# RMS norms in a two-layer diffusion backbone: the last square summed by TensorE, and the roots spread with the identity as moving operand

## The chip, the cores and the metric

The kernel runs on one core of one Trainium2 chip. The metric is the device time of one execution in microseconds (us), lower is better.

## The reference, cut to what matters

The reference is a two-layer backbone over 512 latent tokens and 256 context tokens of 1024 features. Layer 0 mixes tokens with multi-scale retention (4 heads), layer 1 with neighbourhood attention (latent tokens only at its end), and each layer ends in a gated convolutional feed-forward network. What this change touches are the norms:

```
def _rmsnorm(x, w):
    y = x * rsqrt(mean(x * x, axis=-1, keepdims=True) + NORM_EPS)
    return y * w

h  = _rmsnorm(x, norm1_w[i]) * (1 + sc1) + sh1        # before the mixer, each layer
h2 = _rmsnorm(x, norm2_w[i]) * (1 + sc2) + sh2        # before the feed-forward, each layer
o  = o * rsqrt(mean(o * o, axis=-1) + NORM_EPS)       # in retention, once per head
return _rmsnorm(x, final_norm_w)                      # the output
```

That is nine norms: one at the start, four in the retention heads, and four of the residual stream further on.

## The kernel before, in words

Features lie on the partitions and tokens along the free axis, so `x` is 8 tiles of 128 features by 768 tokens (512 latent, then 256 context), and only the 512 latent columns are worked on from the attention's output projection on. A norm has to add squares over all 1024 features of a token, which is a sum over tiles and then over partitions.

All five queues are written out by hand, with semaphores between them. TensorE multiplies weights that arrive as 512 KB chunks. Each chunk is split by ScalarE (`w_hi`, line 804) and VectorE (`w_lo`, line 1169) into a high and a low part, and every product is three matmuls (high by high, high by low, low by high), in the format fp32r. The norm's own matmuls are plain fp32, and one such matmul shows as two weight loads and two matmuls in the trace.

A norm of the residual stream runs so:

1. When TensorE has finished output tile m (0 to 7), VectorE adds it to `x` (`add_gated`, line 1336, or line 1722 in the attention), ScalarE squares it (`final_square`, line 842, into `S[m % 2]`), and VectorE adds the square to `ss` (`add_square`, line 1195). Between these, both engines split a weight chunk for the next products.
2. After the eighth square is added, TensorE multiplies each 128-token block of `ss` with two columns of ones (`token_sums`, line 427), so that a token's sum stands on the token's own partition: `sums`, 2 columns per block, in the fourth bank of `o_ps`.
3. ScalarE takes the square root (`root`, line 830). Ahead of it a dummy activation (line 827) loads the table, so that the load doesn't wait for the sums.
4. VectorE takes the reciprocal (`one_over`, line 1201) and multiplies it into copies of the identity (line 1202), which makes `ss` a row of 128x128 diagonal matrices, 6 or 4 of them.
5. TensorE multiplies ones (128x128, stationary) by these diagonals (`spread_roots`, line 434): a matmul of 512 columns and, where context is included, one of 256. Every partition then holds the root of every token (`spread`).
6. VectorE multiplies `x` by it (line 1313, or 1734 in the final norm), ScalarE adds the shift and rounds (line 873), VectorE makes the low part (line 1322), and the first tile of the next products can start (line 448).

The four norms of this kind are called A (after retention's output projection), B (after the first feed-forward), C (after the attention's output projection, 512 tokens) and D (the output's, 512 tokens). The start norm and the four head norms use `add_squares` for all squares and the same steps 2 to 5. In a head, step 5 stands inside a running product: TensorE does it ahead of the fourth of eight blocks of `project_at(0, ...)`. At the start, ScalarE copies `spread` back to `ss` (line 848), and VectorE alternates between dot products for the modulation (lines 1216, 1218) and the norm's work.

In the first feed-forward VectorE also makes the second layer's modulation vectors (`ada_step`, line 1285, one or two after each output tile; `take_ada`, line 1292).

Of the kernel before, what the change touches and what calls it, by code (L numbers as in the profile page):

```python
# [37 lines left out]
P = 128  # L38
# [98 lines left out]
def backbone(nc, x_in, weights, ada_first, ada, cond_rows, small_in, bias_in, masks_in, park, out):  # L137
    ctx = ExitStack()
    with ctx:
# [99 lines left out]
        sq_done, sq_added = sem("sq_done"), sem("sq_added")  # L239
        sums_done, root_done, diag_done, spread_done = sem("sums_done"), sem("root_done"), sem("diag_done"), sem("spread_done")  # L240
        norm_t, h_hi_done, h_lo_done = sem("norm_t"), sem("h_hi_done"), sem("h_lo_done")
# [117 lines left out]
        def _(pe):  # L359
# [70 lines left out]
            def spread_roots(parts):  # L430

                pe.wait_ge(diag_done, diags.up())
                for c0, cn, _ in parts:
                    mm = nc.tensor.matmul(spread[:, c0:c0 + cn], ones[:, :], ss[:, c0:c0 + cn], start=True, stop=True)  # L434
                mm.then_inc(spread_done, 1)

            def project_two(parts, ready, tiles=None):
# [327 lines left out]
            out_projection(True)  # L765
            token_sums(KC, TOK)
            spread_roots(PARTS)
            ffn(PARTS)
            token_sums(KC, TOK)
            spread_roots(PARTS)  # L770
# [10 lines left out]
            h_split.up(KC)  # L781
            token_sums(KC, LAT)
            spread_roots(LATENT)
            ffn(LATENT)
            token_sums(KC, LAT)
            spread_roots(LATENT)
# [3 lines left out]
        def _(act):  # L790
# [187 lines left out]
            def ffn(layer, parts, ends):  # L978
                width = parts[-1][0] + parts[-1][1]
                for n, size in enumerate(GROUPS):  # L980
# [19 lines left out]
                    for m in range(2):  # L1000
                        t, after = wait_after()
                        split()
                        if last:
                            final_square(t, after, 0, m, width)
                    pairs = 2 if ends and last else 3
                    with turns(act, pairs, A.steps(2) + [(raws[0], 16), (raws[1], 16), (squares_added, 2 * last)]) as i:
                        for m in range(2):
                            t, after = wait_after()
                            split()
                            if last:  # L1010
                                final_square(t, after, 2 * i + 2, m, width)
                    if pairs == 2:
                        for m in range(2):
                            t, after = wait_after()
                            final_square(t, after, 6, m, width)

# [134 lines left out]
        def _(dve):  # L1151
# [45 lines left out]
            def one_over(width):  # L1197

                t = width // P
                dve.wait_ge(root_done, roots.up())  # L1200
                step(nc.vector.reciprocal(rms[:, 0:t], rms[:, 0:t]))
                nc.vector.tensor_tensor(ss[:, 0:width].rearrange("p (t q) -> p t q", q=P),
                                        ident.rearrange("p (t q) -> p t q", t=1).to_broadcast([P, t, P]),
                                        rms[:, 0:t].rearrange("p (t q) -> p t q", q=1).to_broadcast([P, t, P]),
                                        ALU.mult).then_inc(diag_done, 1)

# [134 lines left out]
            def out_projection(with_ada, first_ada=0, final=False):  # L1341
                if final:
                    step(nc.vector.memset(ss[:, :], 0.0))
                own_done()
                for m in range(KC):
                    add_gated(m, 0, 16, PARTS)
                    if m % 2:
                        split()
                    if final:
                        add_square(m % 2, TOK)  # L1350
                    if m % 2:
                        if m < 2 * with_ada:
                            ada_step(first_ada + m // 2, S[3])

            def rotated(j):
# [145 lines left out]
            def ffn(layer, parts, with_ada, ends):  # L1501
# [4 lines left out]
                for n, size in enumerate(GROUPS):  # L1506
# [33 lines left out]
                    own_done()  # L1540
                    pairs = 2 if ends and n == 2 else 3
                    last = n == len(GROUPS) - 1
                    if last:
                        step(nc.vector.memset(ss[:, :], 0.0))
# [16 lines left out]
                    with turns(dve, pairs, A.steps(2) + steps) as i:  # L1561
# [7 lines left out]
                        if loads:  # L1569
                            take_ada(1, i * loads + nj, loads, conds)  # L1570
                    nj += 3 * loads
                    if pairs == 2:
                        for m in range(2):
                            add_gated(6 + m, layer, 40, parts)
                            add_square(m, w_all)

# [10 lines left out]
            head_attention(0, True)  # L1587
            steps = [(ada_loads, 128), (hi_splits, 16), (own_steps, 19), (squares_made, VC), (ada_made, 8), (decays, 4)]
            steps += [(v_hi_made, TT), (qk_hi_made, 8), (p_hi_made, 7), (gate_hi_made, 4)]
# [126 lines left out]
            for m in range(KC):  # L1716
                if m in (0, 4):
                    dve.wait_ge(x_back[m // 4], 16)
                t, tile = out_tile(m)
                wait_at(t)  # L1720
                xv = x[:, m, 0:LAT].rearrange("p (r c) -> p c r", c=COLS)
                nc.vector.scalar_tensor_tensor(xv, tile.rearrange("p (c r) -> p c r", r=ROWS), mod[:, 1, 16 + m, 0:1], xv,
                                               ALU.mult, ALU.add).then_inc(acc_taken[t], 1)
                if m >= 3:
                    split()
                add_square(m % 2, LAT)
            pads()
# [155 lines left out]
```

## Time and profile before

| | |
|---|---|
| median of 3 runs | 2078.77 us (2076.61 to 2079.49) |
| the profiled execution | 2078.47 us |
| its span, first to last instruction | 2076.4 us |
| mean granted TensorE clock | 0.979 of full |
| TensorE busy | 1982.3 us, 95% of the span |
| VectorE busy | 1342.3 us, 65% |
| ScalarE busy | 755.6 us, 36% |
| GpSimd busy | 97.1 us, 5% |

The 2.07 us between the span and the execution's time lie ahead of and behind the instructions. The granted clock is 1.00 at 2.4 GHz and 0.50 at 1.2 GHz. Times in the rows count from the start of the span.

### The profile page before, as it was taken

The page shows a single profiled execution, that of the slowest core. Times are in us where ns is not written, and L with a number is a line of the kernel's source. Part 1 is how long each engine was busy: PE and PEld are TensorE (multiplying, and loading weights), DVE is VectorE, ACT ScalarE, POOL GpSimd, SP SyncE. Part 2 cuts the span into 40 slices and gives each one's busy share as a digit, 9 for nine tenths or more (in the row PEclk, how much of TensorE's full clock was granted, in tenths as well). Part 3 has the DMA queues.
Part 4 walks back from the last instruction along what each step waited for, and adds up shares of the span by engine and source line. Part 5 has one row for each costly group of instructions (what it writes and reads, how often), then busy time and mean ns, then how long its engine had stood idle before and what let it go on. Part 6 is the DMA issues. An engine that isn't in the chain of part 4 may idle for free.

```text
span 2076.4 us, 29858 instructions
## 1 busy us (share of the span) xinstructions
PE 1982.3 (95%) x10452; PEld 1687.3 (81%) x10452; DVE 1342.3 (65%) x2251; ACT 755.6 (36%) x1281; POOL 97.1 (5%) x162
## 2 busy tenths in 40 slices
PE   5999999999999889999999999899999889999997
PEld 4878888888888778888888887688888768788785
DVE  7866635735745677766664667777877667557375
ACT  4423223223313344312321233456556444333232
POOL 0000000000000000000000000311111000000000
PEclk8999999999999989999999999899999989999999
DMA  7221311321221112233224334211111222223222
GB/s 291 90 83 62 112 61 52 106 68 62 92 81 61 61 59 93 91 132 105 97 101 132 101 101 152 89 46 42 56 45 35 92 71 94 98 91 101 91 91 101
DMA packets 51256, 186.39 MB, mean 90 GB/s; under 512 B 5680, under 2 KB 5680, under 8 KB 51184
## 3 DMA queue, kind: packets, MB, share of 16 engines
q1 hardware_dynamic: 37744, 136.73, 19.4%
q0 software_dynamic: 13440, 48.63, 7.0%
q8 instruction: 53, 0.87, 0.2%
q14 instruction: 19, 0.16, 0.0%
HBM read 181.15 MB, written 4.19 MB: 89 GB/s over the span
## 4 chain that ended last, share of the span: by engine, by line
PE 83%; DVE 9%; issue 4%; ACT 3%; DMA 1%; DVEq 0%; SPq 0%; ACTq 0%
PE acc L393 58%; PE o_ps L483 3%; PE o_ps L518 3%; PE acc L606 3%; PE acc L483 2%; PE o_ps L649 2%; PE acc L664 2%; PE acc L505 2%; PE acc L448 2%; PE o_ps L664 2%; DVE pt_lo L1625 1%; PE acc L639 1%; PE o_ps L434 1%; PE acc L699 1%; DVE w_lo L1169 1%
## 5 line engine op out<-in xcount | busy, mean ns | idle before, releaser
L804 ACT ACTIVATE w_hi<-raw 128x1024 fp32r<-128x1024 f32 x232 | 245.2, 1057 | 597.5 <-PE acc L393 477.6
L1169 DVE TENSOR_TENSOR w_lo<-raw,w_hi 128x1024 fp32r<-128x1024 f32 x232 | 284.2, 1225 | 275.4 <-ACT w_hi L804 273.9
L393 PE MATMUL acc<-h_hi,w_hi 128*128 128x512 f32 x1520 | 437.5, 351 | 4.9 <-DVE w_lo L1169 3.4
L393 PE MATMUL acc<-h_hi,w_lo 128*128 128x512 f32 x1520 | 434.5, 349 | 0.0
L393 PE MATMUL acc<-h_lo,w_hi 128*128 128x512 f32 x1520 | 434.1, 349 | 0.0
L393 PEld LDWEIGHTS acc<-h_hi,w_hi 128*128 128x128 f32 x1520 | 245.2, 188 | 44.4 <-ACT u L990 4.2
L393 PEld LDWEIGHTS acc<-h_lo,w_hi 128*128 128x128 f32 x1520 | 245.0, 188 | 39.6
L393 PEld LDWEIGHTS acc<-h_hi,w_lo 128*128 128x128 f32 x1520 | 243.9, 188 | 38.7
L1336 DVE SCALAR_TENSOR_TENSOR x<-acc,mod,x 128x512 f32<-128x512 f32 (+3 forms) x136 | 81.9, 637 | 145.1 <-PE acc L393 135.7
L393 PE MATMUL acc<-act_hi,w_lo 128*128 128x512 f32 (+1 forms) x396 | 119.8, 356 | 0.0
L393 PE MATMUL acc<-act_hi,w_hi 128*128 128x512 f32 (+1 forms) x396 | 119.5, 356 | 0.0
L393 PE MATMUL acc<-act_lo,w_hi 128*128 128x512 f32 (+1 forms) x396 | 119.3, 355 | 0.0
L1285 DVE CUSTOM_DVE_ANT_0 ada_raw<-ada_raw,silu_rows 128x1024 f32<-128x1024 f32 x80 | 97.9, 1223 | 4.9 <-DMA ada_raw<-in_ada_dram 2.8
L312 POOL DMA_DIRECT2D ada_raw<-in_ada_dram x79 | 41.8, 529 | 1180.0 <-DVE mod_new L1285 1180.0
L997 ACT ACTIVATE act_hi<-scratch 128x768 f32 (+1 forms) x44 | 32.5, 740 | 154.2 <-DVE scratch L1529 154.2
L1520 DVE SCALAR_TENSOR_TENSOR scratch<-u,taps,scratch 128x769 f32<-128x769 f32 (+1 forms) x88 | 78.0, 887 | 3.1
L1522 DVE SCALAR_TENSOR_TENSOR scratch<-u,taps,scratch 128x769 f32<-128x769 f32 (+1 forms) x88 | 78.0, 887 | 3.1
L1625 DVE TENSOR_TENSOR pt_lo<-acc,pt_hi 128x256 fp32r<-128x256 f32 (+1 forms) x128 | 52.3, 450 | 35.3 <-ACT pt_hi L1065 35.2
L393 PEld LDWEIGHTS acc<-act_lo,w_hi 128*128 128x128 f32 x396 | 65.0, 187 | 12.1
L393 PEld LDWEIGHTS acc<-act_hi,w_lo 128*128 128x128 f32 x396 | 65.0, 187 | 12.0
L393 PEld LDWEIGHTS acc<-act_hi,w_hi 128*128 128x128 f32 x396 | 65.0, 187 | 11.9
L1535 DVE TENSOR_TENSOR act_lo<-scratch,act_hi 128x768 f32 (+1 forms) x44 | 36.3, 825 | 45.4 <-ACT act_hi L997 45.4
(231 smaller groups left out, 3520.5 us busy)
## 6 DMA issues: line engine op xcount, KB each, us to landing
raw<-in_weights_dram SPq DMA_DIRECT2D x232, 512.0 KB, 3.3
ada_raw<-in_ada_dram POOLq DMA_DIRECT2D x80, 512.0 KB, 3.6
ada_start<-in_ada_first_dram SPq DMA_DIRECT2D x8, 1024.0 KB, 18.3
x<-in_x_in_dram SPq DMA_DIRECT2D x4, 768.0 KB, 7.0
park_dram<-x POOLq DMA_DIRECT2D x1, 2048.0 KB, 8.1
rel<-in_bias_dram POOLq DMA_DIRECT2D x16, 128.0 KB, 2.4
x<-park_dram POOLq DMA_DIRECT2D x2, 1024.0 KB, 6.6
out_dram<-x SPq DMA_DIRECT2D x8, 256.0 KB, 2.1
```

Of the source, the lines that this page charges most:

```text
L393: mm = nc.tensor.matmul(tile[:, c0:c0 + cn], wt[:, b * P:(b + 1) * P], mv[:, n, c0:c0 + cn], start=(n == 0 and m == 0), stop=(n == last an ...
L483: mm = nc.tensor.matmul(tile, hs[:, k, t * P:(t + 1) * P], ws[:, d * RV:(d + 1) * RV], start=(k == 0 and m == 0), stop=(last and m == 2))
L518: mm = nc.tensor.matmul(tile, vt[:, c0:c0 + P], pt[i % 2][:, p0:p0 + qn], start=((context or i == 0) and n == 0 and m == 0), stop=(i >= 5 ...
L606: mm = nc.tensor.matmul(tile[:, c0:c0 + cn], wt[:, n * P:(n + 1) * P], mv[:, n, c0:c0 + cn], start=(n == 0 and m == 0), stop=(n == size - ...
L664: mm = nc.tensor.matmul(tile[:, c0:c0 + cn], wt[:, n * P:(n + 1) * P], mv[:, n, c0:c0 + cn], start=(n == 0 and m == 0), stop=(n == KC - 1 ...
L804: nc.scalar.activation(w_hi[i][:, :], raw[i][:, :], ACT.Copy).then_inc(hi_split, 1)
L1169: nc.vector.tensor_tensor(w_lo[i][:, :], raw[i][:, :], w_hi[i][:, :].bitcast(F32), ALU.subtract)\
L1285: nc.vector.tensor_tensor_reduce(ada_raw[:, :], ada_raw[:, :], silu_rows[:, 0, :], 1.0, 0.0, ALU.mult, ALU.add, mod_new[:, j, 0:1]).then_i ...
L1336: ins = nc.vector.scalar_tensor_tensor(xv, tile[:, c0:c0 + cn], mod[:, layer, bass.ds(gate + m, 1), c:c + 1].rearrange("p a c -> p (a c)") ...
L1520: step(nc.vector.scalar_tensor_tensor(S[j][:, 0:width], u[j][:, 1:1 + width], tap(1), S[j][:, 0:width], ALU.mult, ALU.add))
L1522: nc.vector.scalar_tensor_tensor(S[j][:, 0:width], u[j][:, 2:2 + width], tap(2), S[j][:, 0:width], ALU.mult, ALU.add).then_inc(conv_done, 1)
L1625: ins = nc.vector.tensor_tensor(lo, tile[:, c0:c0 + zn * P].rearrange("p (t q) -> p t q", q=P), hi.bitcast(F32), ALU.subtract)
```

## The change: what it does

In norms A to D the eighth square is no longer added to `ss`. The new `final_sums` takes the place of `token_sums`: TensorE waits for seven additions and multiplies `ss` with ones (first batch, 6 or 4 matmuls), and then waits for ScalarE's eighth square and multiplies `S[1]` with ones on top, into the same PSUM columns (second batch, as many again). TensorE itself raises `sq_added` in place of the addition that went.

In all nine norms the diagonals are gone. `spread_roots` waits for the reciprocal alone, and does one matmul for each 128-token block: stationary is the block's column of reciprocals, repeated 128 times by a stride of zero, moving is the 128x128 identity. The columns multiplied are as many as before (768 or 512), in 6 or 4 matmuls in place of 2 or 1.

In the last group of both feed-forwards, output tiles 6 and 7 are written out behind the loop, in VectorE's and ScalarE's queues alike, with the same steps in the same order but for the addition that went.

```diff
             def spread_roots(parts):
-                pe.wait_ge(diag_done, diags.up())
-                for c0, cn, _ in parts:
-                    mm = nc.tensor.matmul(spread[:, c0:c0 + cn], ones[:, :], ss[:, c0:c0 + cn], start=True, stop=True)
+                pe.wait_ge(roots_ready, diags.up())
+                for t in range((parts[-1][0] + parts[-1][1]) // P):
+                    mm = nc.tensor.matmul(spread[:, t * P:(t + 1) * P], rms[:, t:t + 1].to_broadcast([P, P]), ident,
+                                          start=True, stop=True)
                 mm.then_inc(spread_done, 1)
+
+            def final_sums(width):
+                pe.wait_ge(sq_added, squares_added.up(KC) - 1)
+                for t in range(width // P):
+                    mm = nc.tensor.matmul(sums[:, 2 * t:2 * t + 2], ss[:, t * P:(t + 1) * P], ones[:, 0:2],
+                                          start=(t == 0), stop=False)
+                mm.then_inc(sq_added, 1)
+                pe.wait_ge(sq_done, squares_added.now())
+                for t in range(width // P):
+                    mm = nc.tensor.matmul(sums[:, 2 * t:2 * t + 2], S[1][:, t * P:(t + 1) * P], ones[:, 0:2],
+                                          start=False, stop=(t == width // P - 1))
+                mm.then_inc(sums_done, 1)
...
-            token_sums(KC, TOK)
+            final_sums(TOK)
             spread_roots(PARTS)
...
                 dve.wait_ge(root_done, roots.up())
-                step(nc.vector.reciprocal(rms[:, 0:t], rms[:, 0:t]))
-                nc.vector.tensor_tensor(ss[:, 0:width].rearrange("p (t q) -> p t q", q=P),
-                                        ident.rearrange("p (t q) -> p t q", t=1).to_broadcast([P, t, P]),
-                                        rms[:, 0:t].rearrange("p (t q) -> p t q", q=1).to_broadcast([P, t, P]),
-                                        ALU.mult).then_inc(diag_done, 1)
+                nc.vector.reciprocal(rms[:, 0:t], rms[:, 0:t]).then_inc(roots_ready, 1)
...
-                    if final:
+                    if final and m < KC - 1:
                         add_square(m % 2, TOK)
...
-                    pairs = 2 if ends and n == 2 else 3
+                    pairs = 2 if last else 3
...
-                    if pairs == 2:
+                    if last:
                         for m in range(2):
                             add_gated(6 + m, layer, 40, parts)
-                            add_square(m, w_all)
+                            if not ends:
+                                split()
+                            if m == 0:
+                                add_square(m, w_all)
+                            if loads:
+                                ada_step(m, waste, conds)
```

## Rows read from the trace of the kernel before

**Rows 1.** Page, part 4: the chain that ended last, share of the span by engine.

```profile
PE 83%; DVE 9%; issue 4%; ACT 3%; DMA 1%; DVEq 0%; SPq 0%; ACTq 0%
```

**Rows 2.** Instructions on `ss`: engine, count, duration in ns (min/median/max), span, forms.

```profile
L1195 DVE TENSOR_TENSOR ss<-ss,scratch x32: 681/822/959, 693.9 to 2063.2; 128x768 f32<-128x768 f32 x16, 128x512 f32<-128x512 f32 x16
```

**Rows 3.** Chain in order of time, norm A: start us, us, what.

```profile
718.60 1.12 DVE x L1336 x2
...
720.83 0.96 DVE ss L1195
...
721.84 2.73 PE o_ps L427 x12
...
724.59 0.19 ACT rms L830
...
725.10 0.97 DVE ss L1202
...
726.11 2.94 PE o_ps L434 x4
...
732.77 7.31 PE acc L448 x25
```

**Rows 4.** Timeline, norm A: start us, us, engine, what [idle before <-releaser].

```profile
716.50 0.96 DVE L1195 TENSOR_TENSOR ss<-ss,scratch 128x768 f32<-128x768 f32 x1 [0.96 <-ACT scratch L842]
...
720.64 1.28 ACT L827 ACT_TABLE_LOAD   x1
```

**Rows 5.** Timeline, norm B.

```profile
1293.69 0.84 ACT L842 ACTIVATE scratch<-x 128x768 f32 x1 [0.52 <-DVE x L1336]
...
1297.30 0.17 DVE L1300 SCALAR_TENSOR_TENSOR norm_a<-mod,small 128x16 f32<-128x16 f32 x1 [0.28 <-DVE mod L1292]
...
1300.03 2.93 PE L434 MATMUL o_ps<-ss,ones 128*128 128x512 f32 x4 [1.73 <-DVE ss L1202]
```

**Rows 6.** Timeline, norm C, and then norm D.

```profile
1680.60 1.28 ACT L827 ACT_TABLE_LOAD   x1
...
1684.10 2.07 PE L434 MATMUL o_ps<-ss,ones 128*128 128x512 f32 x2 [1.27 <-DVE ss L1202]
...
2063.16 1.28 ACT L827 ACT_TABLE_LOAD   x1
...
2066.27 2.08 PE L434 MATMUL o_ps<-ss,ones 128*128 128x512 f32 x2 [1.30 <-DVE ss L1202]
```

**Rows 7.** Chain in order of time, start norm.

```profile
21.70 2.94 PE o_ps L434 x4
```

**Rows 8.** Timeline of the first head's norm, weight loads.

```profile
165.50 1.42 PEld L427 LDWEIGHTS o_ps<-ones,ss 128*128 128x128 f32 x12
...
169.27 0.30 PEld L393 LDWEIGHTS acc<-h_lo,w_hi 128*128 128x128 f32 x2
...
169.62 0.31 PEld L393 LDWEIGHTS acc<-h_hi,w_lo 128*128 128x128 f32 x2
...
170.96 0.19 PEld L434 LDWEIGHTS o_ps<-ss,ones 128*128 128x128 f32 x1 [0.24 <-issue]
171.39 0.19 PEld L434 LDWEIGHTS o_ps<-ss,ones 128*128 128x128 f32 x1 [0.24 <-issue]
171.60 0.41 PEld L393 LDWEIGHTS acc<-h_hi,w_hi 128*128 128x128 f32 x2
```

**Rows 9.** Timeline, a group of transposes in the attention.

```profile
1348.02 0.71 PE L639 MATMUL acc<-small,prob 128*128 128x128 f32 x5
```

**Rows 10.** Windows: stretch, us, busy us (x count) of PE, PEld, DVE, ACT, POOL, clock, DMA, GB/s.

```profile
28.00:29.00 1.00, 1.00 (x9) 1.00 (x9) 1.00 (x1) 0.00 (x0) 0.00 (x0) 0.77 1.03 410
...
721.00:722.00 1.00, 0.16 (x1) 0.16 (x1) 0.92 (x8) 0.99 (x2) 0.00 (x0) 0.72 0.00 0
...
738.00:739.00 1.00, 1.00 (x7) 0.85 (x6) 1.00 (x3) 0.70 (x2) 0.00 (x0) 0.74 0.00 0
...
1683.00:1684.00 1.00, 0.00 (x0) 0.00 (x0) 0.82 (x2) 0.04 (x1) 0.00 (x0) 1.00 0.92 365
```

More of the change, by code:

```diff
@@ L239, in backbone @@
         sq_done, sq_added = sem("sq_done"), sem("sq_added")
-        sums_done, root_done, diag_done, spread_done = sem("sums_done"), sem("root_done"), sem("diag_done"), sem("spread_done")
+        sums_done, root_done, roots_ready, spread_done = sem("sums_done"), sem("root_done"), sem("roots_ready"), sem("spread_done")
         norm_t, h_hi_done, h_lo_done = sem("norm_t"), sem("h_hi_done"), sem("h_lo_done")
@@ L765, in _ @@
             out_projection(True)
-            token_sums(KC, TOK)
+            final_sums(TOK)
             spread_roots(PARTS)
             ffn(PARTS)
-            token_sums(KC, TOK)
+            final_sums(TOK)
             spread_roots(PARTS)
@@ L781, in _ @@
             h_split.up(KC)
-            token_sums(KC, LAT)
+            final_sums(LAT)
             spread_roots(LATENT)
             ffn(LATENT)
-            token_sums(KC, LAT)
+            final_sums(LAT)
             spread_roots(LATENT)
@@ L1004, in ffn @@
                             final_square(t, after, 0, m, width)
-                    pairs = 2 if ends and last else 3
+                    pairs = 2 if last else 3
                     with turns(act, pairs, A.steps(2) + [(raws[0], 16), (raws[1], 16), (squares_added, 2 * last)]) as i:
@@ L1353, in out_projection @@
                             ada_step(first_ada + m // 2, S[3])
+                if final:
+                    squares_made.up()
             def rotated(j):
@@ L1540, in ffn @@
                     own_done()
-                    pairs = 2 if ends and n == 2 else 3
                     last = n == len(GROUPS) - 1
+                    pairs = 2 if last else 3
                     if last:
@@ L1570, in ffn @@
                             take_ada(1, i * loads + nj, loads, conds)
-                    nj += 3 * loads
-                    if pairs == 2:
+                    nj += pairs * loads
+                    if last:
                         for m in range(2):
                             add_gated(6 + m, layer, 40, parts)
-                            add_square(m, w_all)
+                            if not ends:
+                                split()
+                            if m == 0:
+                                add_square(m, w_all)
+                            if loads:
+                                ada_step(m, waste, conds)
+                        if loads:
+                            take_ada(1, nj, loads, conds)
+                        nj += loads
+                        squares_made.up()
             def pads():
@@ L1587, in _ @@
             head_attention(0, True)
-            steps = [(ada_loads, 128), (hi_splits, 16), (own_steps, 19), (squares_made, VC), (ada_made, 8), (decays, 4)]
+            steps = [(ada_loads, 128), (hi_splits, 16), (own_steps, 18), (squares_made, VC), (ada_made, 8), (decays, 4)]
             steps += [(v_hi_made, TT), (qk_hi_made, 8), (p_hi_made, 7), (gate_hi_made, 4)]
@@ L1725, in _ @@
                     split()
-                add_square(m % 2, LAT)
+                if m < KC - 1:
+                    add_square(m % 2, LAT)
+            squares_made.up()
             pads()
```

## The prediction

> **What bounds the kernel now.** I read the page first: TensorE, busy 95% of the span by the table above, holds 83% of the chain that ended last, VectorE 9% [rows 1]. So time is won only where TensorE stands still or does less, and VectorE's 9% are where it stands still. Next I listed the instructions on `ss`, the tile that the edit touches: four of 32 additions close a norm [rows 2], and all nine diagonals stand between a root and a spread. Then I read the chain at each norm. In norm A it is a relay with no slack: the eighth addition, 12 weight loads and matmuls for the sums, root, reciprocal, diagonals, spread [rows 3]. From the last product, which released VectorE at 718.60, to the end of the spread at 729.05 TensorE does nothing but these small matmuls, the later ones at half clock: the 12 of the sums take 2.73 us, where the same 12 in a head take 1.42 [rows 3, 8], and the granted clock fell in the window 721 to 722, at 721.44 by its mean of 0.72 [rows 10].
>
> **The prices.** A weight load with a matmul of two columns costs 1.42 / 12 = 0.118 us at full clock and 2.63 / 12 = 0.219 at half (the 2.73 less the last matmul's tail) [rows 3, 8]. The new spread does 12 loads, each with 128 moving columns, which the trace before doesn't show in plain fp32. Its matmul part follows from the old spread: loads 170.96 and 171.39 are one 512-column matmul apart, 0.43 us, so 128 columns are 0.107, or 0.213 at half clock [rows 8]. The load is the longer of the two. If it runs under the matmul ahead of it, 12 cost 12 x 0.118 = 1.42 us (0.219 each, 2.63, at half clock); if the two follow one another, 12 x 0.225 = 2.70 (5.18). I take the first. Transposes of the same shape, a load and 128 fp32 columns, stand (0.71 - 0.27) / 4 = 0.11 us apart, with 0.27 for the last one's own duration [rows 9]. And the old spread's third load went in at 170.96 just as the second matmul began.
>
> A rule speaks against this. The Trainium skill, "TensorE: Matmul & The Clock Gate", section "Measured speedup vs the span model", has weight loads overlapping with matmuls in flight "only when row_grp differs", and here all use the whole array. By that the second price would hold; this trace's rows for transposes speak for the first. I keep it as a rival below.
>
> **The change part by part.** Each term is a shift of the moment at which the spread is ready, against the profiled execution.
>
> *Start norm.* VectorE goes from the reciprocal to the diagonals (the size of A's, 0.97 us [rows 3]), TensorE's spread of 2.94 starts at 21.70 [rows 7], and ScalarE's copy and all that follows hang on it. The spread runs at the half-clock pace and stays at it: 12 x 0.219 + 0.3 for the tail = 2.93. The gain is the diagonal, 0.95. It is kept: the chain goes on from the spread through ScalarE's copy and then through VectorE, which has work without a gap for the rest of this norm. Between 0.9 and 1.0.
>
> *Heads, four times.* The product's weight loads come 0.35 us apart per pair (169.27, 169.62), so the next would be at 169.97. It came at 171.60: 1.63 us for the wait on the diagonals and the spread [rows 8]. The old wait ended by 170.5; without the diagonal it would end at about 169.5, before TensorE comes by. There is no wait left, and 1.42 for the loads: 0.21 saved, 0.85 over four heads. Ends 0.6 and 1.0, for loads 0.005 us further apart or closer.
>
> *First batch of the sums.* In A the seventh addition ended at 717.46, before the last product, which released VectorE at 718.60 [rows 3, 4]; the order in B, C and D is the same. The batch takes 1.42 (C and D 0.94) on an engine that waits for the eighth square anyway. In A that ends where the table load begins, 720.64 [rows 4]. Nothing is paid; without that cover it would be 1.42.
>
> *Norm A, addition and sums.* The second batch starts when the square ends, at some 720.7, not at 721.84. Its price depends on when the clock falls. At the old moment (721.44, from the 0.72) it does about six at 0.118 and six at 0.219, 2.0, and the root starts at 722.75 in place of 724.59. ScalarE allows 722.15: table load from 720.64 to 721.92, then the dummy's 0.2 [rows 4]. From root to spread there were 0.48 us for root and reciprocal, 0.97 for the diagonals and 0.04; now 0.53. Spread at 723.3 in place of 726.11 [rows 3]: 2.8 saved, and the spread itself is a draw at half clock. Ends: second batch wholly slow, 2.1; all at full clock, root 722.15, spread at 722.7 and 1.7 long in place of 2.94, 4.6.
>
> *Norm B.* The square ends at 1294.53. The batch needs about 2.3 with the clock falling soon after its start: root 1297.0, spread 1297.55 in place of 1300.03 [rows 5], 2.5 saved. A new limit lies close: VectorE still has its modulation step, now 0.96 earlier since the addition ahead of it is gone, and ends line 1300 at 1296.5 in place of 1297.47 [rows 5]. The reciprocal is queued behind it. This binds only if the sums run at full clock. Ends 2.2 and 4.4.
>
> *Norms C and D.* Here ScalarE binds: square, table load, dummy, root. The load ends at 1681.88 and 2064.44, the root can start 0.2 later, at 1682.1 and 2064.65, and the batch (8 x 0.118 = 0.94 behind a square that ends as the table load starts) is done by then. Spreads start at 1682.65 and 2065.2 in place of 1684.10 and 2066.27 [rows 6]: 1.45 and 1.05. Both old spreads ran at half clock (2.07, 2.08 us). The new ones are 8 x 0.118 + 0.3 = 1.24 if they come before the fall and 2.05 if after. At the old phase both would be fast: in C the granted clock was 1.00 through the window 1683 to 1684 [rows 10], in which the new one ends, and in D the old one starts 0.1 us after the new one ends. But A's fall at 721.4, 2.8 us after its product, shows that the phase differs. I take one of the two as fast: 1.45 + 1.05 + 0.83 = 3.3. Ends 2.5 and 4.15.
>
> The rest costs nothing: the written-out tiles 6 and 7 have the same steps, and ScalarE's and VectorE's splits for the next products lie where they did. Nothing waits anew on GpSimd or SyncE; their transfers are released by the same events, a few us earlier.
>
> **Sum.** 0.95 + 0.85 + 2.8 + 2.5 + 3.3 = 10.4 us. The profiled execution would go from 2078.47 to 2068.1; it stands 0.3 under the median, so the median would go from 2078.77 to 2068.4. The low ends add up to 0.9 + 0.6 + 2.1 + 2.2 + 2.5 = 8.3 (2070.5), the high ends to 1.0 + 1.0 + 4.6 + 4.4 + 4.15 = 15.2 (2063.6).
>
> **The rivals.**
>
> *Weight loads and matmuls in series.* In every spread each record costs 0.107 more at full clock and 0.213 at half: start, A and B 36 x 0.213 = 7.7, C and D 16 x 0.213 = 3.4, heads 48 x 0.107 = 5.1; 16.2 in all. 10.4 saved less 16.2 is 5.8 lost: 2084.6, slower. It eats the whole gain from 64% of that price on (10.4 of 16.2), and is slower by 0.2% from 90% on. For it speaks only that no plain fp32 load with 128 columns is in the trace, and that its operand is one column repeated; against it stand the transposes [rows 9]. That overlap which the skill's section denies is this rival.
>
> *The clock does not fall.* TensorE works wide again about 4.4 us after its last product, not 7.5 us. If that is enough in A, B, C and D, the terms reach their high ends, 2063.6. The products after the norm would also start at full clock. In A they began at 732.77 and the clock rose only in the window 738 to 739, at 738.5 by its mean of 0.74 [rows 3, 10]: of 5.7 us half is lost, 2.9. VectorE, which makes the tiles in step with them, would keep about half of that back; 1.5 remain in A and as much in C: down to 2060.6. Against it: two-column matmuls did not hold the clock at the start, where it fell in the window 28 to 29 with TensorE busy throughout [rows 10], and from the spread's end to the products another 3.7 us went by (729.05 to 732.77) [rows 3].
>
> *The gain is given back.* The clock's fall is not tied to the kernel. If it comes earlier relative to each norm, the second batches are slow, and if the rise afterwards comes later by 1 to 2 us in A and C, half of that is lost as well: 5 to 7 us saved in all, 2072 to 2074. For it: in A the rise came 5.7 us after the products began, so there is room for another phase of it.
>
> *Within the measurement.* The change does what it says, but a partly hidden load, 6 to 14 us in all, eats the gain: about 2078.
>
> **How the numbers follow.** The forecast gets 0.64, the clock that stays 0.14, the gain given back 0.10, the partly hidden load 0.05, the series 0.07. A measurement of this kernel can tell 0.2%, 4.2 us, from no change. Faster by more: 0.64 + 0.14 + 0.10 = 0.88; within: 0.05; slower: 0.07. Predicted are 2068.4 us. The range must leave no more than 2 in 10 out. It takes the low-gain side to 2073.0, most of the gain given back, and the other to 2062.0, most of the clock that stays.
>
> **What would show each step.** After the change there are 28 additions on `ss` in place of 32, and no diagonal. In a head the spread's 12 weight loads stand 0.12 us apart with no idle time ahead of them; 0.22 apart means the series rival. In A, 12 sums begin before the square, and the root starts near 722.7 less the 1.8 us gained until then. In C and D the root follows the dummy at once. The windows tell whether the spreads came before the clock's fall. What would make the prediction wrong is above all the price of the load with a repeated column; next the clock's phase, worth up to 1.2 us for each of A and B and 0.8 for C and D.

## The result, and the profile after

The changed kernel takes 2063.7 us, median of 4 (2061.64 to 2064.35); the kernel before, beside it on the same chip, 2078.43, median of 4 (2076.61 to 2079.49). The ratio is 0.9928, 95% interval 0.9911 to 0.9946: faster by 14.7 us. Predicted were 2068.4 us within 2062.0 to 2073.0. A repeat of the same kernel on another chip, below, gave 11.9 us (0.9946, 0.9933 to 0.9959). The two intervals overlap, so the gain is known as 12 to 15 us and not closer.

The page of the changed kernel, parts 1 and 4 (busy us by engine; chain by engine, against [rows 1]):

```profile
PE 1982.4 (96%) x10560; PEld 1699.1 (82%) x10560; DVE 1331.9 (65%) x2238; ACT 755.3 (37%) x1281; POOL 97.1 (5%) x162
...
PE 83%; DVE 9%; issue 4%; ACT 2%; DMA 1%; DVEq 0%; SPq 0%; ACTq 0%; POOLq 0%
```

TensorE is busy for the same 1982 us as before in a span of 2062.2 instead of 2076.4 us: on balance what went is idle time. (The four first batches were added to its busy time, and stretches at full clock that ran at half before took as much away.) VectorE lost 10.4 us of work. The shares of the chain hardly move, so they tell nothing about which wait went. The mean granted clock of the two profiled executions rose from 0.979 to 0.987. Instructions on `ss`, against [rows 2]:

```profile
L1211 DVE TENSOR_TENSOR ss<-ss,scratch x28: 678/822/960, 693.2 to 2046.2; 128x768 f32<-128x768 f32 x14, 128x512 f32<-128x512 f32 x14
```

Four additions are gone, and no diagonal is left. Timeline of the first head's norm, against [rows 8]:

```profile
169.67 0.30 PEld L393 LDWEIGHTS acc<-h_hi,w_lo 128*128 128x128 f32 x2
...
170.02 1.42 PEld L434 LDWEIGHTS o_ps<-small,rms 128*128 128x128 f32 x12
170.13 1.50 PE L434 MATMUL o_ps<-small,rms 128*128 128x128 f32 x12
171.36 0.30 PEld L393 LDWEIGHTS acc<-h_hi,w_hi 128*128 128x128 f32 x2
```

Twelve loads in 1.42 us, 0.118 each, with no idle time ahead, although 128 moving columns follow each load: loads and matmuls overlap. From the product's last loads ahead of the spread to the first behind it 1.69 us pass (169.67 to 171.36), and 1.98 passed before (169.62 to 171.60): 0.29 saved. The Trainium skill's sentence that weight loads overlap with matmuls in flight "only when row_grp differs" ("TensorE: Matmul & The Clock Gate", section "The mechanism"; the section that the prediction names is the one behind it) doesn't hold for these rows: every load here uses the whole array, and 12 loads with 128 columns each took 1.42 us and not 2.70.

The first batch of the sums in norm A:

```profile
717.57 1.42 PEld L442 LDWEIGHTS o_ps<-ones,ss 128*128 128x128 f32 x12
```

It follows the last product's loads at once and has ended at 718.99, 0.97 us before the second batch may start; in B, C and D it starts at 1286.20, 1667.81 and 2048.49 and is done before the square too. It costs nothing, as predicted.

Chain in order of time at norm A, against [rows 3]:

```profile
717.89 1.15 DVE x L1348 x2
...
719.07 0.85 ACT scratch L856
...
719.96 1.51 PE o_ps L447 x12
...
721.50 0.19 ACT rms L844
...
721.77 0.20 DVE rms L1217
...
722.02 2.94 PE o_ps L434 x12
```

The second batch follows the square at once and takes 1.51 us, tail included: all of it at full clock. The root follows it, the spread follows the reciprocal, and the spread runs at half clock. From the last product's release (717.89) to the spread's end (724.97 by the chain) 7.08 us pass; before it was 10.45 (718.60 to 729.05).

Chain in order of time at norm C:

```profile
1670.07 1.69 PE o_ps L447 x8
...
1671.77 0.18 ACT rms L844
...
1672.28 2.09 PE o_ps L434 x8
```

and at norm D, where line 841 is the table load:

```profile
2050.41 1.28 ACT L841
...
2051.90 0.07 ACT rms L844
...
2052.33 1.87 PE o_ps L434 x8
```

In C the second batch is on the chain and partly slow, so the root waits for it and not for the table load; in D the table load is on it, as predicted. Both spreads are at or near the half-clock time of [rows 6].

The same reading at each place (start us; "shift" is after less before, counted from the start of the span; "own" is the change of the shift over the norm itself):

| place | before | after | shift | own |
|---|---|---|---|---|
| start norm's spread ends | 24.64 | 23.73 | -0.91 | -0.91 |
| first products' chain after it | 79.28 | 79.42 | +0.14 | |
| last product before A taken by VectorE | 718.60 | 717.89 | -0.71 | heads -0.85 |
| A: spread ends | 729.05 | 724.97 | -4.08 | -3.37 |
| last product before B taken by VectorE | 1292.35 | 1286.52 | -5.83 | |
| B: spread ends | 1302.97 | 1294.41 | -8.56 | -2.73 |
| last product before C taken by VectorE | 1678.81 | 1668.24 | -10.57 | |
| C: spread ends | 1686.19 | 1674.37 | -11.82 | -1.25 |
| last product before D taken by VectorE | 2061.68 | 2048.93 | -12.75 | |
| D: spread ends | 2068.36 | 2054.20 | -14.16 | -1.41 |

"Taken" is the moment at which VectorE starts on the product. That is 0.02 us after its end everywhere but before B in the kernel before: there the product ended at 1292.09 and VectorE came 0.24 us late. Counted from the product's end, B's own step is 2.97 and the stretch between A and B gave 1.51. The changed kernel, with tiles 6 and 7 written out behind the loop, has no such delay; no run separates the cause.

The own steps from the heads on sum to 0.85 + 3.37 + 2.73 + 1.25 + 1.41 = 9.6 us. The other 4.6 of the 14.2 us arise in places that the edit doesn't touch: 1.75 between A and B, 2.0 between B and C, 0.9 between C and D, less 0.14 lost ahead of the heads. Windows of the changed kernel (columns as in [rows 10]):

```profile
60.00:62.00 2.00, 2.00 (x6) 1.52 (x6) 1.93 (x5) 1.76 (x2) 0.00 (x0) 0.50 0.00 0
...
721.00:722.00 1.00, 0.46 (x5) 0.37 (x4) 0.19 (x1) 0.59 (x3) 0.00 (x0) 0.70 0.60 180
...
731.00:732.00 1.00, 1.00 (x5) 0.86 (x5) 1.00 (x3) 0.02 (x1) 0.00 (x0) 0.68 0.00 0
...
1329.00:1330.00 1.00, 1.00 (x9) 0.95 (x8) 0.97 (x2) 0.31 (x1) 0.00 (x0) 1.00 0.67 193
```

and of the kernel before, two stretches that its rows above did not show:

```profile
60.00:62.00 2.00, 1.48 (x7) 1.26 (x8) 1.97 (x4) 1.97 (x4) 0.00 (x0) 1.00 0.00 0
1329.00:1330.00 1.00, 0.99 (x2) 0.83 (x3) 0.76 (x1) 0.95 (x3) 0.00 (x0) 0.51 0.79 311
```

In A the clock falls at 721.4 by its mean of 0.70 and rises at 731.64 by its mean of 0.68: 3.0 us after the products start at 728.68, where before it rose 5.75 us after (738.52 against 732.77, [rows 3, 10]). After the spread's end the shift grows from 4.08 to 5.62 us within 25 us. In the attention of before the clock fell as the products of line 664 began. Chain there, before:

```profile
1329.01 7.35 PE o_ps L664 x24
```

and after:

```profile
1320.48 5.74 PE o_ps L678 x24
```

The same 24 products took 1.6 us less at 1.00 throughout, which is most of the 2.0 us between B and C. At 60 us it is the other way round: the changed kernel ran at half clock with TensorE busy throughout where the old one ran at full clock, and its backlog of products ate the start norm's 0.91.

### The profile page after: what moved, and what is told of

It reads as the page before. It is cut to its first block, busy times and chain, and to the rows that moved or that the text cites. A ratio compares the mean times of both kernels' runs of the same rounds, so it can differ in the third digit from the quotient of the medians.

```text
span 2062.2 us, 30027 instructions
## 1 busy us (share of the span) xinstructions
PE 1982.4 (96%) x10560; PEld 1699.1 (82%) x10560; DVE 1331.9 (65%) x2238; ACT 755.3 (37%) x1281; POOL 97.1 (5%) x162
## 4 chain that ended last, share of the span: by engine, by line
PE 83%; DVE 9%; issue 4%; ACT 2%; DMA 1%; DVEq 0%; SPq 0%; ACTq 0%; POOLq 0%
PE acc L393 58%; PE o_ps L497 3%; PE o_ps L532 3%; PE acc L620 3%; PE acc L497 2%; PE o_ps L663 2%; PE acc L678 2%; PE acc L519 2%; PE acc L462 2%; PE o_ps L678 1%; DVE pt_lo L1648 1%; PE acc L653 1%; PE acc L713 1%; PE o_ps L434 1%; DVE w_lo L1185 1%
```

## The experiments

Four questions: does each half of the edit give its own steps; is the overlap real; how much of the gain is the clock; and what limits what is left. The runs stand in three groups (halves, doubled heads and first filling; delays, more filling and norm B; repeats, narrow filling and filling without the change). Those of one group share a chip and its runs of the kernel before, whose medians were 2077.81 (10 runs, 2073.89 to 2079.36), 2075.95 (17, 2072.15 to 2079.3) and 2076.91 (11, 2071.67 to 2079.63).

### Each half alone

Sums by two batches, diagonals and old spread kept:

```
-                pe.wait_ge(roots_ready, diags.up())
-                for t in range((parts[-1][0] + parts[-1][1]) // P):
-                    mm = nc.tensor.matmul(spread[:, t * P:(t + 1) * P], rms[:, t:t + 1].to_broadcast([P, P]), ident, ...)
+                pe.wait_ge(diag_done, diags.up())
+                for c0, cn, _ in parts:
+                    mm = nc.tensor.matmul(spread[:, c0:c0 + cn], ones[:, :], ss[:, c0:c0 + cn], start=True, stop=True)
```

> The sums of norms A to D as changed (last square by TensorE), the diagonals and the old spread kept. Both theories take the shortened steps themselves from the two traces: 2.4 us in A, 1.7 in B (VectorE's modulation step limits it), 0.55 in C, 0.45 in D, 5.1 in all. Theory 'steps': that is all, 2073.3 us; what the full change gained beyond its steps (14.7 us measured, 9.6 in steps) is chance of the clock's phase. Theory 'clock follows': TensorE idles for less time, so it spends less time at half clock, and this kernel gains 7 us or more, 2071.4 or less, with a mean granted clock above 0.979.

2070.36 us, median of 6 (2067.02 to 2072.4), ratio 0.9966 [0.9954, 0.9978]: 7.45 us saved.

The identity as moving operand, with the eighth addition kept:

```
-            final_sums(TOK)
+            token_sums(KC, TOK)
```

> The identity spread in all nine norms, the sums as before. The steps: four heads 0.86 us together, A 0.97, B 1.0, C and D 0.7 each, 4.2 in all; the start norm's 0.95 is had earlier but lost again if the clock falls there as in the changed kernel. Theory 'steps': 2074.2 us, or 2073.3 with the start's part. Theory 'clock follows': 6 us or more gained, 2072.4 or less, and with the sums-only kernel the two gains add up to the full change's 14.7.

2069.33 us, median of 5, ratio 0.9957 [0.9943, 0.9970]: 8.5 us saved. Together 15.9 us, against the full edit's 14.7 and 11.9. Both halves carry a share, and neither needs the other. Against the steps' 5.1 and 4.2 they lie 2.4 and 4.3 us higher; with intervals of about 2.5 us either way only the second excess is outside them.

### Does a load run under a matmul?

The spread done twice in each head, 48 more records of a load and 128 columns:

```
-                for t in range((parts[-1][0] + parts[-1][1]) // P):
+                for t in times * list(range((parts[-1][0] + parts[-1][1]) // P)):
...
-                project_at(0, lambda n: spread_roots(PARTS) if n == 3 else None)
+                project_at(0, lambda n: spread_roots(PARTS, 2) if n == 3 else None)
```

> The changed kernel with the six spread matmuls done twice in each of the four heads, where TensorE is never idle. It prices the load with a repeated column. If loads run under the matmuls: 12 x 0.118 = 1.42 us more per head, 5.7 in all, 2069.4 us. If load and matmul were in series: 2.7 per head, 10.8 in all, 2074.5 us.

2069.14 us, median of 5, ratio 0.9958 [0.9944, 0.9972]. That is 5.4 us over the changed kernel's 2063.7 and 4.1 over its 2065.05 in the repeat. Timeline of its first head, weight loads:

```profile
170.38 2.76 PEld L434 LDWEIGHTS o_ps<-small,rms 128*128 128x128 f32 x24
```

24 loads in 2.76 us, 0.115 each. In series they would take 24 x 0.225 = 5.4 us. That rival is out, by the row rather than by the total.

### Where the phase of the clock stands

Some 1.5 us of idle fills of a spare tile on VectorE in the start norm shift all that follows, in the kernel before and in the changed one:

```
                 scale(0)
+                for _ in range(2):
+                    step(nc.vector.memset(S[3][:, 0:TOK], 0.0))
                 one_over(TOK)
```

> The kernel before with two idle memsets of 0.70 us (1.5 us with their waits) on VectorE in the start norm's relay, and nothing else. Theory 'phase is chance, and before had a bad one': the whole program shifts by 1.5 us, the clock's falls land elsewhere, and the time may even drop: 2075 to 2081 us. Theory 'clock follows the idle time': idle time is as long as before, the half-clock stretches are as many, and the time is the 2078 us of before plus up to 1.5: 2078 to 2079.5.

2076.71 us, median of 12 (2072.98 to 2080.55), ratio 1.0006 [0.9997, 1.0015]. The median doesn't move clear of noise, and the run doesn't tell the theories apart: 2076.71 lies in the first one's 2075 to 2081, and 0.8 over the 2075.95 beside it lies in the second one's 0 to 1.5. Single executions of the unchanged kernel range over 2071.67 to 2079.63 in the three groups, so a fixed delay needn't add anything to what varies already. (In this run's profiled execution, 2072.98 us, the clock reads 0.95 wherever others read 1.00, and 0.933 in the mean, although it is the shortest of the twelve. No run explains that, and nothing here rests on it.)

> The changed kernel with the same 1.5 us of delay in the start norm. In the changed kernel the start norm's own gain (0.9 us) was lost until the first head, to a stretch at half clock. Theory 'start is hidden': TensorE's backlog swallows the delay too, 2064 us, no later than 2064.5. Rival 'the start norm is on the path': 2065.2 us. If the changed kernel owed 4 us to a lucky phase, this one goes back to 2068.

2065.78 us, median of 5 (2064.03 to 2067.07), ratio 0.9950 [0.9935, 0.9964], 0.7 over the repeat of the changed kernel on another chip (below). Too little to tell whether a delay at the start is hidden or not: inconclusive. On its own chip it is 10.2 us under the kernel before, and 10.9 under that kernel with the same delay. So the run gives the full 11.9 us no support against the 9.6 of own steps, and doesn't exclude it: the interval of its ratio is 7.5 to 13.5 us.

### Keeping the clock up

Idle matmuls of 256 columns into a spare corner of `o_ps`, two between the batches of the sums and six after each spread of A, B and C. All outputs are computed as before:

```
+            def keep_busy(count):
+                for _ in range(count):
+                    nc.tensor.matmul(o_ps[:, 2, 0:256], ident, small[:, 0:256], start=True, stop=True)
...
                 mm.then_inc(sq_added, 1)
+                keep_busy(2)
                 pe.wait_ge(sq_done, squares_added.now())
...
             spread_roots(PARTS)
+            keep_busy(6)
             ffn(PARTS)
```

> The changed kernel with idle work for TensorE in the gaps of norms A to D: two plain fp32 matmuls of 256 columns after the first batch of sums (0.86 us at full clock), and six after the spread of A, B and C (2.6 us at full clock, 5.1 at half). If it is the idle gaps that make the clock fall, it stays up: spreads 1.2 us shorter in A and B, 0.8 in C and D, and the products after A and C begin at full clock and save 1.3 and 1.5: up to 6.8 us gained, 2057 us. If the clock falls all the same, the six run at half clock, end 1.4 us after the products could have begun, and A and C lose that: 2066.5 us. VectorE paces the products in B, so B's own loss is hidden.

2058.43 us, median of 4 (2057.11 to 2059.54), ratio 0.9911 [0.9895, 0.9926]. Mean clock 0.993. Its chain at norm A:

```profile
718.18 0.97 PE o_ps L441 x4
719.16 1.42 PE o_ps L453 x12
...
720.60 0.19 ACT rms L853
...
720.88 0.20 DVE rms L1226
...
721.12 1.62 PE o_ps L434 x12
...
726.46 5.58 PE acc L468 x29
```

and a window of the same stretch:

```profile
721.00:722.00 1.00, 0.88 (x7) 0.88 (x8) 0.07 (x1) 0.00 (x0) 0.00 (x0) 1.00 0.89 365
```

The spread takes 1.62 us instead of 2.94, and the products after it start at full clock. In C the clock fell all the same. Chain there, with the filling:

```profile
1668.93 2.08 PE o_ps L434 x8
1671.00 3.15 PE o_ps L441 x12
1674.15 10.34 PE acc L468 x45
```

and the changed kernel's piece for the same products:

```profile
1676.90 12.19 PE acc L462 x45
```

The spread took as long as the old one ([rows 6]), and the filling ran at half clock and past the moment at which the products could have begun. But the products behind it took 1.85 us less. From the last product before C to the end of these 45 it is 19.26 us with the filling (1665.23 to 1684.49) and 20.85 without (1668.24 to 1689.09), so it gained 1.6 in C as well.

The repeat of this version beside a repeat of the changed kernel:

> The changed kernel once more, unaltered, on the chip of the runs beside it. The kernel before alone has ranged from 2072 to 2079 us over 27 executions by now, so its first median (2078.4 of 4) may have been high. If half of the 4.6 us beyond the steps was that, the ratio comes nearer to 1 than 0.9928: 0.994, near 2065 us. If none was, 0.993 and 2063.7.

2065.05 us, median of 5 (2063.66 to 2066.1), ratio 0.9946 [0.9933, 0.9959]: 11.9 us.

> The kernel with TensorE's idle work in norms A to D once more, on the same chip as the unaltered changed kernel. By the runs so far, on different chips, it is 5 us faster than that. If it holds, 2058.4 us.

2058.95 us, median of 5 (2054.86 to 2060.31), ratio 0.9911 [0.9896, 0.9926]: 6.1 us faster than the changed kernel on the same chip. The two intervals don't touch. This version is faster than both kernels.

More of it, one or two after the second batch, five ahead of the queries' weights and five ahead of the wait in the output projection:

```
                 mm.then_inc(sums_done, 1)
+                keep_busy(1 if width == TOK else 2)
...
                     outputs(NP - 1)
+                    keep_busy(5)
                     pe.wait_ge(no_taken, NP + 1)
```

> The kernel with idle work of the last call and more of it: one more fp32 matmul of 256 columns after the second batch in A and B, two in C and D, five (2.1 us) before the first wait for the queries' weights and five before the wait at the start of the attention's output projection, where the clock fell for 3 to 4 us each. If the falls go away: C's products save 3.0 (its filler at half clock and its first products), D's spread 0.8 less, the two places 1.6 and 1.6 each: 2058.4 less up to 5, 2053.5 us. If falls only move to the next gap: 2058 us.

2057.4 us, median of 5 (2056.91 to 2060.31), ratio 0.9914 [0.9899, 0.9929]: no more than the smaller filling gives. The falls moved rather than went: the first filling's windows show half clock at 1317 to 1321 and 1648 to 1652 us, where this one has none, and this one's show it at 1611 to 1615, 1686 to 1690 and 2014 to 2018, where the other has none. Its norm C still ran slow, from the spread on:

```profile
1667.48 1.71 PE o_ps L434 x8
1669.19 2.80 PE o_ps L441 x12
```

### Is it the width or the work?

The same with 2 columns instead of 256, and more of them (4 and 11), so that TensorE is as occupied:

```
-                    nc.tensor.matmul(o_ps[:, 2, 0:256], ident, small[:, 0:256], start=True, stop=True)
+                    nc.tensor.matmul(o_ps[:, 2, 0:2], ident, small[:, 0:2], start=True, stop=True)
```

> The same idle work with two columns in place of 256, and more of it, so that TensorE is occupied as long: four matmuls in place of two after the first batch (0.94 us at full clock by the weight loads), eleven in place of six after the spread (2.6 us). Theory: what holds the clock is wide matmuls, as at the start, where it fell in the middle of a stream of two-column matmuls. Then the clock falls as in the changed kernel, 2064 us, or up to 2 us later where the eleven run at half clock (4.8 us) and end after the products could begin. Rival: any occupation of TensorE holds it, 2058.4 us.

2065.44 us, median of 6 (2062.03 to 2067.78), ratio 0.9943 [0.9930, 0.9956], the changed kernel's own gain and nothing on top. Windows at norm A:

```profile
719.00:720.00 1.00, 0.86 (x8) 0.78 (x7) 0.00 (x0) 0.91 (x3) 0.00 (x0) 0.90 0.51 61
721.00:722.00 1.00, 1.00 (x7) 1.00 (x6) 0.00 (x0) 0.00 (x0) 0.00 (x0) 0.50 0.48 193
```

TensorE is busy in all of 721 to 722 and stands at 0.50; with wide matmuls the same window was busy for 0.88 us at 1.00. So the busy column alone doesn't tell at which level the clock stands.

### The fill without the change

The kernel before with idle matmuls of 256 columns: six ahead of the sums, three between sums and spread, six after the spreads of A, B and C.

```
+            keep_busy(6)
             token_sums(KC, TOK)
+            keep_busy(3)
             spread_roots(PARTS)
+            keep_busy(6)
             ffn(PARTS)
```

> The kernel before with idle work and without the change: in norms A to D six fp32 matmuls of 256 columns ahead of the sums, three between sums and spread, and in A, B and C six after the spread. It tells what of the gain the clock alone can give. Sums in A and B take 1.3 us less, all spreads 1.2 or 0.8 less, products after A and C 1.3 to 1.5 less: 9 us at most, 2068 us. If idle work is of use only with the shortened relay, 2077 us.

2068.2 us, median of 6 (2065.73 to 2071.47), ratio 0.9961 [0.9947, 0.9974]: 8.7 us saved with every step of the relay in place. Its chain at norm A:

```profile
721.26 0.96 DVE ss L1211
...
722.27 1.51 PE o_ps L427 x12
...
724.31 0.97 DVE ss L1218
...
725.33 1.57 PE o_ps L434 x4
```

Sums and spread run at full clock, addition and diagonals stand where they stood. With a filling (a smaller one) and the change, on the same chip, 2058.95: 9.2 us between the two medians (10.4 by the ratios), with the mean clock at 0.993 in both. That is about what the edit is worth with the clock all but equal, and it agrees with the 9.6 us of own steps read from the traces, as far as intervals of some 3 us can say. The changed kernel gained 14.7 and 11.9 us, so 2.7 to 5.5 us beyond 9.2 would be the clock's; with the 10.4 of the ratios and the repeat's 11.9 only 1.5, which these intervals don't tell from nothing.

### The limit that is left in B

The last of the 80 modulation dot products left out and its wait for the transfer moved behind norm B, so one column of the modulation is not computed:

```
-                            if loads:
+                            if loads and m == 0:
                                 ada_step(m, waste, conds)
+                            elif loads:
+                                ada_loads.up(16)
+                                nc.vector.tensor_copy(mod_new[:, 7, 0:1], lift[:, 0:1]).then_inc(ada_used, 1)
+                                ada_made.up()
```

> The changed kernel without the last dot product of the second layer's modulation (one of 80; its column of the modulation is not computed), and with the wait for its transfer moved behind the spread of norm B. In B the root was done at 1290.31 and the reciprocal began at 1291.22, behind that step, which itself waited 0.72 us for its transfer. Theory: that queue is B's new limit, and B becomes 0.9 us shorter; if the clock then still stands when the spread begins (it fell 0.2 us into it), the spread takes 1.3 less: 2062.8 to 2061.5 us. Rival, the sums or ScalarE bound B anyway: 2063.7.

2062.69 us, median of 6 (2061.6 to 2067.18), ratio 0.9942 [0.9927, 0.9957], which the total can't tell from the changed kernel's 0.9946. The trace can. Timeline of norm B in the changed kernel:

```profile
1288.59 1.42 PEld L447 LDWEIGHTS o_ps<-ones,scratch 128*128 128x128 f32 x12 [0.96 <-ACT scratch L856]
...
1289.55 1.23 DVE L1297 CUSTOM_DVE_ANT_0 ada_raw<-ada_raw,silu_rows 128x1024 f32<-128x1024 f32 x1 [0.72 <-DMA ada_raw<-in_ada_dram]
...
1290.13 0.18 ACT L844 ACTIVATE rms<-o_ps 128x6 f32<-128x6 f32 x1
...
1291.22 0.19 DVE L1217 RECIPROCAL rms<-rms 128x6 f32<-128x6 f32 x1
1291.47 2.63 PEld L434 LDWEIGHTS o_ps<-small,rms 128*128 128x128 f32 x12 [1.47 <-DVE rms L1217]
```

and the chain of norm B without that step:

```profile
1289.75 0.18 ACT rms L844
...
1290.28 2.42 PE o_ps L434 x12
```

In the changed kernel the root is done at 1290.31 and the reciprocal starts at 1291.22, 0.91 us later, behind the modulation step, which itself waited 0.72 us for its transfer. Without it, 4.14 us pass from the last product's release (1286.14) to the spread's start, against 4.95 (1286.52 to 1291.47): 0.8 us of the 0.9 that were expected. The spread took 2.42 us instead of 2.94, 0.5 less where up to 1.3 was expected: the clock fell during it.

## Why the prediction was right

**The price of the spread** held: 0.118 us per load with 128 columns at full clock, 2.94 us for 12 at half clock. The series rival (2084.6 us) is excluded by the head's rows and by the doubled heads. The partly hidden load is excluded with it.

**The heads** gave 0.28 to 0.30 us each where 0.21 was taken, 1.17 in all. Some 0.3 of it was given back between the heads, in small steps that were not followed further, so that 0.85 arrived at A: the predicted total, by luck, since 0.21 was too little for each and nothing was taken off between them.

**Norm A**: 3.37 where 2.8 was taken, within its ends. The term that was mis-sized is the second batch. It was taken as "about six at 0.118 and six at 0.219, 2.0" and took 1.51. The root starts 3.09 us earlier (721.50 against 724.59), 0.71 of it brought along from the heads and 2.38 won here, where 1.84 was taken. The fall, at 721.4, came as the batch ended. The clock fell at the same moment as before, but the whole norm had moved 0.7 us ahead of it. The spread was at half clock, as said.

**Norm B**: 2.73 where 2.5 was taken. The VectorE limit that the prediction named is there, and it binds with the sums at full clock, as stated. The sums were taken as slow and ran at full clock (1.50 us), the limit took 0.91 of that back, and 2.73 is what is left of the two. That a transfer stands behind the limit was not seen: the step moved up with the missing addition and then waited 0.72 us for its data.

**Norms C and D**: 1.25 and 1.41, 2.66 together, where 1.45 + 1.05 + 0.83 = 3.3 was taken. The term behind "I take one of the two as fast", 0.83, is the one that failed: C's spread took 2.09 us, D's 1.87 where both old ones took 2.09 by the chain, so 0.2 came of it. "At the old phase both would be fast" was not sound for D either: 2065.2 and 1.24 make 2066.44, behind the old spread's start at 2066.27 and the old fall at 2066.3 (window 2066 to 2067, mean 0.65). The clock fell during C's sums and during D's spread. C's sums (1.69 us instead of some 0.94) came out from behind the table load and cost 0.2 of the 1.45: the spread started 4.04 us after the last product instead of 5.29 (1.25). In D it was 3.40 instead of 4.59 (1.19, where 1.05 was taken). The profiled execution of the repeat shows how much of this is the clock's phase: there D's spread took 1.27 us, at full clock, C's 2.09, and the two norms gave 1.60 + 2.01 = 3.6, so one of the two was fast as predicted.

**The start norm**: its 0.95 came (0.91 at the spread) and was lost before the first products. The argument that VectorE "has work without a gap for the rest of this norm" stopped too early: who uses the norm is TensorE. The chain of the changed kernel runs through TensorE alone from 59.61 us to the products at 79.42, as that of the old one does from 60.52 to 79.28. Its first 12 records, in the stretch at half clock, took 4.38 us instead of 2.97: that is more than VectorE had won. In the repeat the spread ended 1.23 us earlier than before, the clock fell in the same stretch (mean 0.69 in the window 60 to 62), and nothing was left at 79.29. No run was made to take the fall away there.

**What was missing from the sum** is the clock outside the norms: 4.6 us between the norms in the profiled execution. The prediction had the mechanism, but only inside the rival "the clock does not fall", where it put 1.5 us on A and as much on C. Measured were 1.5 right after A and 0.9 after C although the clock did fall, because it rose sooner after the products' start, and 1.6 in the attention, which no step had. The two errors have opposite signs: own steps 9.6 instead of 10.4, the clock elsewhere 4.6 instead of 0. By the own steps alone the median would have been 2068.8, as forecast. The measured 2063.7 stands near the fast end of the range, at the sum of all high ends (2063.6) and in the room kept for the rival "the clock does not fall". It got there with falls in every norm and with time won at other places: that part of the hit is luck.

How much of the clock's share returns can be read from the repeat's profiled execution (2064.51 us). Its chain after norm A, in the attention and in norm D:

```profile
726.80 17.49 PE acc L462 x90
...
1319.13 7.33 PE o_ps L678 x24
...
2053.24 1.27 PE o_ps L434 x8
```

The 1.6 us in the attention are chance: the same kernel took 7.33 us there this time, as long as the kernel before, and the two executions with the same filling took 7.33 and 5.72. Right behind norm A the gain returned: the 90 products took 18.75 us before, 17.22 in the changed kernel and 17.49 in its repeat. Norms A to D gave 9.5 us of own steps in the repeat (3.37, 2.48, 1.60, 2.01) and 8.8 in the first profile.

The clock did rise with the change, by less than the two profiles say. Taken over all executions on record, the mean granted clock of the kernel before is 0.982 in each of the three groups (single executions 0.979 to 0.985), and that of the changed kernel 0.987 over 4 and 0.986 over 5 (0.982 to 0.988). The halves had 0.986 and 0.985. What this rise is worth in time beyond the shortened steps stays open between nothing and some 5 us; the delays of the start did not separate it.

## What to carry to other kernels

When an engine's idle gap is a relay between engines, price the edit twice: by the steps that leave the relay, and by the clock of the stretch behind it; here the first was worth 9 to 10 us of the 12 to 15, and the second the rest, of which only the 1.3 to 1.5 us behind norm A were seen twice. Where TensorE must wait, a few wide idle matmuls in the gap can be worth as much as the relay's shortening (8.7 against 9.2 us here), and the two add up for the most part (18.0 us together). When a step is moved up in a queue, look at when the data of every later step in that queue arrives, as in B.

## What the runs showed that was not expected

- A TensorE that is busy throughout can stand at half clock. With narrow matmuls TensorE was busy for the whole window 721 to 722 at a clock of 0.50; with 256-column ones it was busy for 0.88 of it at 1.00.
- A stationary operand that is one column repeated 128 times loads as fast as a dense one: 0.115 to 0.118 us per load, against 0.118 for `ss` blocks [rows 8].
- Filling a gap removes a fall in one place and it may return in another: with more fill the clock still fell at norm C (1.71 us for 8 records, 2.80 for 12), and the total did not improve (2057.4 against 2058.43 and 2058.95, on three chips).
- A fall of the clock seen in one profile and not in another needn't be the edit's: in the attention the same kernel had it in one execution and not in the next, worth 1.6 us.
- Executions of the kernel before lie between 2071.67 and 2079.63 us over 38 runs on three chips, nearly twice the bound of 4.2 us taken for the measurement. A single pair of executions would not have told 5 us from nothing.
